# Value stage of a product-key layer: 640 instead of 512 columns gathered, and one subtraction moved from VectorE to GpSimd

## The chip, the cores and the metric

The kernel runs on one core of a Trainium2 chip. The core has TensorE (PE, matrix products), VectorE (DVE), ScalarE (ACT), GpSimd (POOL, which here also issues the indirect DMAs), SyncE (SP, which issues the plain DMAs) and 16 DMA engines. The metric is the device time of one execution in microseconds, lower is better.

## The reference

The whole program is one gMLP block, one stick-breaking attention block, one mixer of convolution and mLSTM, and at the end a layer with product keys ("PEER"), for 256 tokens of width 2048 in float32. The change touches only the last part, the value side of that layer:

```python
def peer_ffn(h, wq, keys, u, v):            # u, v: (N_EXPERTS = 16384, D = 2048)
    ...                                      # 8 heads x 16 experts are chosen for each token
    gate = jax.nn.softmax(top_s, axis=-1)
    ue = jnp.take(u, eid, axis=0)
    act = jax.nn.gelu(jnp.einsum('thkd,td->thk', ue, xt), approximate=False)
    ve = jnp.take(v, eid, axis=0)
    return jnp.einsum('thk,thkd->td', gate * act, ve)
```

Each token thus adds 128 rows of the value table `v`, each with its own weight `gate * act`. Then `h = layernorm(ALPHA * h + ff)` is the output.

## The kernel before

The first 2560 us or so are the earlier blocks, the choice of experts and the gather of rows of `u` (the "ring stage", line 564 for the gathers and line 1853 for the dot products). The weights are then scattered with one-hot matrices (lines 929 and 1840) into a dense table `wT`, 256 tokens by 16384 experts. What follows is called the value stage here.

The value stage splits the 2048 columns of `v` in two. The first 1536 (`V_DENSE`) go through TensorE: the whole table is streamed in 128 chunks of 128 experts, and each chunk is multiplied with the 128 experts' column of `wT`. The last 512 (`V_GATHERED`) are gathered: for each token the 128 chosen rows, one pick at a time for 128 tokens, which VectorE multiplies by the weight and adds.

TensorE has fp32r products (float32 operands rounded to fewer bits), so each operand is used as a rounded part and the rest, and a chunk is three products for each of two token tiles: rounded weights by rounded values, rest of the weights by rounded values, rounded weights by rest of the values. With three banks of 512 columns these are 18 matmuls. Weights and values of even and odd chunks have two buffers (slot `s`).

Each engine's work for chunk c, with the functions' names:

- SP, `load_v`: two transfers of 128 x 768 from the table into `v_raw`, each once the same half of chunk c - 2 was subtracted (`v_lo`).
- ScalarE, `round_w` (waits until TensorE is done with chunk c - 2, then line 1228 writes the rounded weights) and `round_v` (line 1235, two halves).
- VectorE, in `stream_v`: `lo_w` (line 1931, rest of the weights, 128 x 256, two inputs), then twice `lo_v` (line 1938, rest of half a chunk of values) and `weigh` (line 1917, one gathered pick; even picks are added into `h`, odd ones into `v_odd`). Two picks go with one chunk, so that 256 picks (2 tiles of 128) end with the 128 chunks. After every eight picks `stage` (line 1825) copies the next eight row numbers into `idx`.
- GpSimd: the gathers of line 578, each into one of four `v_rows`, once the pick four before it has been weighed (`v_used`). It reads its row numbers from `idx`. After the first tile it also loads two rows of parameters (1 MB each).
- TensorE, `multiply_v` (line 945), waits for `w_hi` and `v_hi`, after six matmuls for `w_lo`, after twelve for `v_lo`.

Each engine executes its own queue in the order in which it is written, so an instruction that waits holds all behind it on that engine. After the last chunk VectorE adds what TensorE has summed (line 1967), and the layer norm ends the kernel.

Of the kernel before, what the change touches and what calls it, by code (L numbers as in the profile page):

```python
# [41 lines left out]
D = 2048  # L42
# [21 lines left out]
GROUP_HEADS = 2  # L64
TILE_GROUPS = PEER_HEADS // GROUP_HEADS
GROUP_PICKS = GROUP_HEADS * TOPK
V_PARTS = 4
V_GATHERED = D // V_PARTS
V_DENSE = D - V_GATHERED
V_BANKS = V_DENSE // BANK  # L70
V_SLOTS = 4
V_HALVES = 2
V_HALF = V_DENSE // V_HALVES
# [70 lines left out]

def build(nc, x, norm_g, a_w_in, a_v_norm_g, a_w_s, a_b_s, a_w_out, b_w_in, b_w_out, final_g, ln_in_g_2, ln_in_b_2,
          w_in_2, b_gate_2, conv_w_2, conv_b_2, mh_norm_g_2, w_out_2, ln1_g_2, ln1_b_2, peer_wq_2, peer_keys_2,
          peer_u_2, peer_v_2, ln2_g_2, ln2_b_2, out):
    NTH, FILL = number_units()
    FIRST, CHUNKS = number_chunks()

# [1 line left out]
    with ctx:  # L152
# [284 lines left out]
        @block.sync  # L437
        def _(sp):
            for b in range(2):
                cut = slice(b * COLS, (b + 1) * COLS)  # L440
                sp.dma_start(h[:, :, cut], x[0].rearrange("(t p) d -> p t d", p=P)[:, :, cut])\
                    .then_inc(loaded[f"x{b}"], 16)

            def load_block(w, c, col, kts=KT):
                for k in range(kts):
                    if not (isinstance(c, int) and c + k < RAW_SLOTS):

                        sp.wait_ge(split_done, c + (k + 1 - RAW_SLOTS))
                    sp.dma_start(w_raw[:, k % RAW_SLOTS, :], w[k * P:(k + 1) * P, bass.ds(col, COLS)])\
                        .then_inc(raw_landed[k % RAW_SLOTS], 16)  # L450

            def load_pairs(w, stage, col, pairs):
                c = FIRST[stage + "0"]
                with sp.Fori(0, pairs) as i:
                    for n in range(2):
                        load_block(w, i * (2 * KT) + (c + n * KT), i * (2 * COLS) + (col + n * COLS))

            for n in range(4):
                load_block(a_w_in[0], FIRST[f"gmlp_v{n}"], GMLP_W + n * COLS)
            load_pairs(a_w_in[0], "gmlp_u", 0, 2)  # L460
            load_pairs(a_w_in[0], "gmlp_z", 2 * GMLP_W, 2)
            for n in range(2):
                load_block(a_w_out[0], FIRST[f"gmlp_out{n}"], n * COLS, 2 * KT)
            load_pairs(b_w_in[0], "att_q", 0, 4)
            load_pairs(b_w_out[0], "att_out", 0, 1)
            for name, (_, b) in MIX_IN.items():
                load_block(w_in_2[0], FIRST[name], b * COLS)
            load_pairs(w_out_2[0], "mix_out", 0, 1)
            load_pairs(peer_wq_2[0], "peer_q", 0, 1)

            def load_v(c, s):

                if s == 1 and isinstance(c, int):

                    sp.wait_ge(scattered, TOKENS // SCATTER + 2)
                for b in range(V_HALVES):
                    cut = slice(b * V_HALF, (b + 1) * V_HALF)
                    if not isinstance(c, int):
                        sp.wait_ge(v_lo, c * V_HALVES + (b + 1 - 2 * V_HALVES))
                    sp.dma_start(v_raw[s][:, cut], peer_v_2[0, bass.ds(c * N_KEYS, N_KEYS), cut])\  # L480
                        .then_inc(v_raw_landed[s][b], 16)

            sp.wait_ge(keys_known, TILES)
            for s in range(2):
                load_v(s, s)
            with sp.Fori(1, N_KEYS // 2) as i:
                for s in range(2):
                    load_v(i * 2 + s, s)
            for n in range(2 * TILES):
                t, b = divmod(n, 2)  # L490
                cols_ = slice(b * COLS, (b + 1) * COLS)
                sp.wait_ge(out_ready, n + 1)
                sp.dma_start(out[0, t * P:(t + 1) * P, cols_], h[:, t, cols_]).then_inc(y_stored, 16)
            sp.wait_ge(y_stored, 2 * 16 * TILES)
# [3 lines left out]
        def _(pool):  # L498
# [54 lines left out]
            with pool.Fori(0, TILES * PICKS // BODY) as i:  # L553
                for n in range(BODY):
# [11 lines left out]
                        in_offset=bass.IndirectOffsetOnAxis(ap=idx[:, b, s:s + 1], axis=0),  # L566
                    ).then_inc(row_landed[s], 16)

            for t in range(TILES):
                with pool.Fori(0, PICKS // BODY) as i:  # L570
                    for n in range(BODY):
                        b, s = divmod(n, GATHER_SLOTS)
                        if s == 0:
                            pool.wait_ge(idx_ready[b], i + ((TILES + t) * PICKS // BODY + 1))

                        pool.wait_ge(v_used, i * BODY + (t * PICKS + n + 1))
                        pool.nop(nofuse=True)
                        nc.gpsimd.indirect_dma_start(  # L578
                            out=v_rows[n % V_SLOTS][:, :], out_offset=None,
                            in_=peer_v_2[0].rearrange("e (s d) -> (e s) d", s=V_PARTS),  # L580
                            in_offset=bass.IndirectOffsetOnAxis(ap=idx[:, b, s:s + 1], axis=0),
                        ).then_inc(v_landed[n % V_SLOTS], 16)
                if t == 0:
                    pool.wait_ge(v_products, D // P)
                    row(row_g2[:, :], ln2_g_2[0], "rows_ln2")
# [4 lines left out]
        def _(pe):  # L590
# [681 lines left out]
        def _(dve):  # L1272
# [620 lines left out]
            for n in range(GROUPS_IN_ALL):  # L1893
# [3 lines left out]
                    keys_of(0)  # L1897
                if n + 2 == GROUPS_IN_ALL:

                    step(v.tensor_scalar(eid[:, ALL:2 * ALL], eid[:, 0:ALL], float(V_PARTS), V_PARTS - 1.0, ALU.mult,  # L1900
                                         ALU.add))
                    step(v.memset(eid[:, 2 * ALL:], 0))
                    keys_of(1)
                finish_gate(n)
# [20 lines left out]
                dve.wait_ge(v_used, (t + 1) * PICKS + V_SLOTS)  # L1925
                step(v.tensor_tensor(h[:, t, V_DENSE:], h[:, t, V_DENSE:], v_odd[:, :], ALU.add))

            def lo_w(c, s):

                dve.wait_ge(w_hi, c + 1)  # L1930
                v.tensor_tensor(w_x[s][:, 1, :, :, :], wT[:, :, bass.ds(c, 1), :], w_x[s][:, 0, :, :, :].bitcast(F32),
                                ALU.subtract).then_inc(w_lo, 1)

            def lo_v(c, s, b):

                cut = slice(b * V_HALF, (b + 1) * V_HALF)
# [8 lines left out]
            def stream_v(t):  # L1945

                with dve.Fori(0, PICKS // BODY) as i:
                    for n in range(BODY // 2):
                        c = i * (BODY // 2) + (t * (N_KEYS // TILES) + n)
                        lo_w(c, n % 2)  # L1950
                        for b in range(V_HALVES):
                            lo_v(c, n % 2, b)
                            weigh(t, i, t * PICKS + 2 * n + b)
# [6 lines left out]


            for t in range(TILES):
                v.bn_stats(bn[:, t, V_BANKS, :], h[:, t, V_DENSE:])
            dve.wait_ge(v_products, N_KEYS)
            for t in range(TILES):
                dst = h[:, t, 0:V_DENSE]
                step(v.scalar_tensor_tensor(out=dst, in0=dst, scalar=ALPHA, in1=flat[t][:, 0:V_DENSE], op0=ALU.mult,
                                            op1=ALU.add))
                for n in range(V_BANKS):
                    ins = v.bn_stats(bn[:, t, n, :], h[:, t, n * BANK:(n + 1) * BANK])  # L1970
                step(ins)
                step(tile_moments(t))
# [12 lines left out]

_INS = ["x", "norm_g", "a_w_in", "a_v_norm_g", "a_w_s", "a_b_s", "a_w_out", "b_w_in", "b_w_out", "final_g", "ln_in_g_2",
        "ln_in_b_2", "w_in_2", "b_gate_2", "conv_w_2", "conv_b_2", "mh_norm_g_2", "w_out_2", "ln1_g_2", "ln1_b_2",
        "peer_wq_2", "peer_keys_2", "peer_u_2", "peer_v_2", "ln2_g_2", "ln2_b_2"]


# [15 lines left out]
```

## Time and profile before

| | |
|---|---|
| median of 3 runs | 3186.89 us (3186.21 to 3187.88) |
| the profiled execution | 3189.3 us, its span 3187.6 us |
| busy over the span | PE 75%, DVE 70%, ACT 35%, POOL 24% |
| value stage | from about 2634 us to 3165 us of the span |
| bytes moved | 766.51 MB, 240 GB/s over the span |

How to read it: PE, DVE, ACT, POOL are the busy times of the engines; a DMA share is the time that packets took on the core's 16 DMA engines as a share of 16 engines' time in that stretch. Queue q1 holds the transfers that SP issues, queue q0 those that GpSimd issues, the gathers among them. The duration of an indirect DMA on POOL is the time that GpSimd spends on issuing it; its time to landing is given apart. Durations of one VectorE operation after another overlap by some 0.1 us, so the cadence is read from their starts. The granted clock of TensorE is 1.00 at its upper level.

### The profile page before, as it was taken

The page shows a single profiled execution, that of the slowest core. Times are in us where ns is not written, and L with a number is a line of the kernel's source. Part 1 is how long each engine was busy: PE and PEld are TensorE (multiplying, and loading weights), DVE is VectorE, ACT ScalarE, POOL GpSimd, SP SyncE. Part 2 cuts the span into 40 slices and gives each one's busy share as a digit, 9 for nine tenths or more (in the row PEclk, how much of TensorE's full clock was granted, in tenths as well). Part 3 has the DMA queues.
Part 4 walks back from the last instruction along what each step waited for, and adds up shares of the span by engine and source line. Part 5 has one row for each costly group of instructions (what it writes and reads, how often), then busy time and mean ns, then how long its engine had stood idle before and what let it go on. Part 6 is the DMA issues. An engine that isn't in the chain of part 4 may idle for free.

```text
span 3187.6 us, 33891 instructions
## 1 busy us (share of the span) xinstructions
PE 2394.3 (75%) x10945; PEld 2000.4 (63%) x10945; DVE 2242.5 (70%) x2950; ACT 1111.3 (35%) x1197; POOL 763.3 (24%) x548
## 2 busy tenths in 40 slices
PE   7999999999999998999998900000111149999997
PEld 5888888888888886888886700000111147887885
DVE  4456455555444556455656699999999998888888
ACT  4444344444444543343443300000000024444443
POOL 1000000000000000000000076665565614455543
PEclk8999999999999998899999955555555589999998
DMA  7655555555656354555564498888897928999996
GB/s 246 195 186 185 178 179 191 185 192 185 185 185 185 124 194 139 164 162 166 187 221 155 172 403 369 362 362 354 316 379 306 391 78 294 320 317 331 322 323 230
DMA packets 183123, 766.51 MB, mean 240 GB/s; under 512 B 22172, under 2 KB 22224, under 8 KB 149104
## 3 DMA queue, kind: packets, MB, share of 16 engines
q1 hardware_dynamic: 123232, 415.29, 40.3%
q0 software_dynamic: 59792, 349.90, 28.0%
q8 instruction: 62, 1.02, 0.1%
q14 instruction: 37, 0.30, 0.0%
HBM read 763.00 MB, written 2.10 MB: 240 GB/s over the span
## 4 chain that ended last, share of the span: by engine, by line
PE 69%; DVE 22%; issue 5%; DMA 2%; ACT 1%; DVEq 1%; POOL 0%; SPq 0%; ACTq 0%; POOLq 0%
PE half L604 50%; PE half L945 15%; DVE ring L1853 14%; DVE onehot_a L1840 2%; PE half L623 1%; DMA w_raw<-in_a_w_in 1%; DMA v_raw<-in_peer_v 1%; DVE onehot_b L1836 1%; PE half L800 1%; DVEq L1840 0%; PE half L672 0%; DMA v_rows<-in_peer_v,idx 0%; DVE left L1751 0%; PE half L903 0%; DVE onehot L1794 0%
## 5 line engine op out<-in xcount | busy, mean ns | idle before, releaser
L604 PE MATMUL half<-w_split,xT 128*128 128x512 f32 x7104 | 1639.0, 392 | 15.2 <-DVE xT L1302 12.6
L604 PEld LDWEIGHTS half<-w_split,xT 128*128 128x128 f32 x7104 | 1337.9, 189 | 294.5 <-issue 8.6
L1283 DVE TENSOR_TENSOR w_split<-w_raw,w_split 128x1024 fp32r<-128x1024 f32 x592 | 722.5, 1225 | 764.1 <-ACT w_split L985 763.3
L985 ACT ACTIVATE w_split<-w_raw 128x1024 fp32r<-128x1024 f32 x592 | 626.6, 1059 | 943.4 <-PE half L604 914.1
L564 POOL DMA_INDIRECT ring<-in_peer_u,idx x256 | 480.9, 1879 | 439.5 <-DVE dots L1853 186.2
L1853 DVE CUSTOM_DVE_ANT_0 ring<-ring,h 128x2048 f32<-128x2048 f32 x256 | 570.0, 2285 | 5.0 <-issue 2.5
L945 PE MATMUL half<-v_split,w_x 128*128 128x512 f32 x2304 | 526.8, 391 | 6.1 <-ACT v_split L1235 4.4
L945 PEld LDWEIGHTS half<-v_split,w_x 128*128 128x128 f32 x2304 | 434.4, 189 | 98.3 <-issue 5.6
L929 PE MATMUL half<-onehot_a,onehot_b 128*128 128x128 f32 x512 | 94.9, 361 | 334.9 <-DVE onehot_a L1840 334.9
L578 POOL DMA_INDIRECT v_rows<-in_peer_v,idx x256 | 266.7, 1042 | 330.2 <-DVE h L1917 208.5
L929 PEld LDWEIGHTS half<-onehot_a,onehot_b 128*128 128x128 f32 x512 | 87.8, 267 | 342.2 <-DVE onehot_a L1840 342.2
L502 POOL DMA_DIRECT2D row_a<-in_final_g x1 | 0.5, 531 | 1130.6 <-DVE ao L1509 1130.6
L1938 DVE TENSOR_TENSOR v_split<-v_raw,v_split 128x768 fp32r<-128x768 f32 x256 | 244.3, 954 | 19.6 <-ACT v_split L1235 19.1
L1235 ACT ACTIVATE v_split<-v_raw 128x768 fp32r<-128x768 f32 x256 | 211.0, 839 | 42.0 <-DMA v_raw<-in_peer_v 39.2
L1219 ACT ACTIVATE wT<-half 128x1024 f32 x32 | 32.8, 1024 | 395.5 <-PE half L929 395.5
L918 PE MATMUL half<-ident,wgt 128*128 128x128 f32 x2 | 0.9, 474 | 186.2 <-DVE wgt L1869 186.2
L918 PE MATMUL half<-ident,pick_keys 128*128 128x128 f32 x4 | 1.0, 354 | 184.1 <-DVE v_odd L1883 184.1
L1228 ACT ACTIVATE w_x<-wT 128x256 fp32r (+1 forms) x128 | 53.4, 418 | 231.4 <-PE half L945 231.4
L918 PEld LDWEIGHTS half<-ident,wgt 128*128 128x128 f32 x2 | 0.4, 182 | 186.8 <-DVE wgt L1869 186.8
L918 PEld LDWEIGHTS half<-ident,pick_keys 128*128 128x128 f32 x4 | 0.6, 175 | 184.3 <-issue 184.3
L1917 DVE SCALAR_TENSOR_TENSOR v_odd<-v_rows,wgt,v_odd 128x512 f32<-128x512 f32 x128 | 95.6, 747 | 16.7 <-DMA v_rows<-in_peer_v,idx 15.8
L1917 DVE SCALAR_TENSOR_TENSOR h<-v_rows,wgt,h 128x512 f32<-128x512 f32 x128 | 95.5, 746 | 7.0 <-DMA v_rows<-in_peer_v,idx 7.0
(287 smaller groups left out, 1152.8 us busy)
## 6 DMA issues: line engine op xcount, KB each, us to landing
w_raw<-in_a_w_in SPq DMA_DIRECT2D x192, 512.0 KB, 3.5
v_raw<-in_peer_v SPq DMA_DIRECT2D x256, 384.0 KB, 5.4
w_raw<-in_b_w_in SPq DMA_DIRECT2D x128, 512.0 KB, 3.5
w_raw<-in_w_in SPq DMA_DIRECT2D x112, 512.0 KB, 3.5
w_raw<-in_a_w_out SPq DMA_DIRECT2D x64, 512.0 KB, 3.5
w_raw<-in_b_w_out SPq DMA_DIRECT2D x32, 512.0 KB, 4.3
w_raw<-in_w_out SPq DMA_DIRECT2D x32, 512.0 KB, 4.6
w_raw<-in_peer_wq SPq DMA_DIRECT2D x32, 512.0 KB, 4.3
```

Source lines behind the costliest of these rows:

```text
L564: nc.gpsimd.indirect_dma_start(out=ring[:, s, :], out_offset=None, in_=peer_u_2[0], in_offset=bass.IndirectOffsetOnAxis(ap=idx[:, b, s:s + ...
L578: nc.gpsimd.indirect_dma_start(out=v_rows[n % V_SLOTS][:, :], out_offset=None, in_=peer_v_2[0].rearrange("e (s d) -> (e s) d", s=V_PARTS), ...
L604: last = mm(ps[half][:, 2 * t + n, :], xt[:, xp, kk, tok], w_split[:, s, wp, n * BANK:(n + 1) * BANK], start=(k == 0 and xp == 0 and wp == ...
L929: last = mm(by_128[s][:, n, :], onehot_b[:, s, n, :], onehot_a[:, s, n, :], start=True, stop=True)
L945: ins = mm(ps[t][:, n, :], w_x[s][:, xp, 1 - t, 0, :], v_split[s][:, vp, n * BANK:(n + 1) * BANK], start=first and xp + vp == 0, stop=last ...
L985: fn(w_split[:, k % SPLIT_SLOTS, 0, :], w_raw[:, k % RAW_SLOTS, :], ACT.Copy).then_inc(hi_done, 1)
L1235: fn(v_split[s][:, 0, cut], v_raw[s][:, cut], ACT.Copy).then_inc(v_hi, 1)
L1283: v.tensor_tensor(w_split[:, s, 1, :], w_raw[:, k % RAW_SLOTS, :], w_split[:, s, 0, :].bitcast(F32), ALU.subtract).then_inc(split_done, 1)
L1840: ins = v.tensor_scalar(onehot_a[:, s, n, :], iota_keys[:, :], picksT[:, 0, bass.ds(token + n, 1)], picksT[:, 2, bass.ds(token + n, 1)], A ...
L1853: v.tensor_tensor_reduce(out=ring[:, s, :], in0=ring[:, s, :], in1=h[:, t, :], scale=1.0, scalar=0.0, op0=ALU.mult, op1=ALU.add, accum_out ...
L1917: v.scalar_tensor_tensor(out=acc, in0=v_rows[m % V_SLOTS][:, :], scalar=wgt[:, bass.ds(i * BODY + m, 1)], in1=acc, op0=ALU.mult, op1=ALU.a ...
L1938: v.tensor_tensor(v_split[s][:, 1, cut], v_raw[s][:, cut], v_split[s][:, 0, cut].bitcast(F32), ALU.subtract).then_inc(v_lo, 1)
```

## The change

640 columns are gathered and 1408 go through TensorE, in banks of 512, 512 and 384 columns. The table is handed to the kernel as two arrays, 1408 and 640 columns wide, where before one array of 2048 columns served both. `lo_w` is taken out of VectorE's loop and written into GpSimd's, behind every second gather.

```diff
-V_PARTS = 4
-V_GATHERED = D // V_PARTS
+V_GATHERED = 640
 V_DENSE = D - V_GATHERED
-V_BANKS = V_DENSE // BANK
+V_BANKS = tuple((lo, min(BANK, V_DENSE - lo)) for lo in range(0, V_DENSE, BANK))
...
-                    sp.dma_start(v_raw[s][:, cut], peer_v_2[0, bass.ds(c * N_KEYS, N_KEYS), cut])\
+                    sp.dma_start(v_raw[s][:, cut], peer_v_dense[0, bass.ds(c * N_KEYS, N_KEYS), cut])\
...
+            def lo_w(c, s):
+
+                pool.wait_ge(w_hi, c + 1)
+                nc.gpsimd.tensor_tensor(w_x[s][:, 1, :, :, :], wT[:, :, bass.ds(c, 1), :],
+                                        w_x[s][:, 0, :, :, :].bitcast(F32), ALU.subtract).then_inc(w_lo, 1)
...
-                            in_=peer_v_2[0].rearrange("e (s d) -> (e s) d", s=V_PARTS),
+                            in_=peer_v_rest[0],
                             in_offset=bass.IndirectOffsetOnAxis(ap=idx[:, b, s:s + 1], axis=0),
                         ).then_inc(v_landed[n % V_SLOTS], 16)
+                        if n % 2:
+                            lo_w(i * (BODY // 2) + (t * (N_KEYS // TILES) + n // 2), n // 2 % 2)
...
-                    for n in range(V_BANKS):
-                        ins = mm(ps[t][:, n, :], w_x[s][:, xp, 1 - t, 0, :], v_split[s][:, vp, n * BANK:(n + 1) * BANK],
+                    for lo, width in V_BANKS:
+                        ins = mm(flat[t][:, lo:lo + width], w_x[s][:, xp, 1 - t, 0, :], v_split[s][:, vp, lo:lo + width],
...
-                    step(v.tensor_scalar(eid[:, ALL:2 * ALL], eid[:, 0:ALL], float(V_PARTS), V_PARTS - 1.0, ALU.mult,
-                                         ALU.add))
+                    step(v.tensor_copy(eid[:, ALL:2 * ALL], eid[:, 0:ALL]))
...
                         c = i * (BODY // 2) + (t * (N_KEYS // TILES) + n)
-                        lo_w(c, n % 2)
                         for b in range(V_HALVES):
                             lo_v(c, n % 2, b)
                             weigh(t, i, t * PICKS + 2 * n + b)
```

GpSimd, the start of the value stage's loop, before (a DMA into `v_rows` is a gather, `v_used` counts weighed picks):

```order
L576 ISA [waits idx_ready0]
L578 DMA v_rows_161<-in_peer_v,idx 128x512 [waits v_used]
L576 REGISTER_ALU
L578 DMA v_rows_162<-in_peer_v,idx 128x512 [waits v_used]
L576 REGISTER_ALU
L578 DMA v_rows_163<-in_peer_v,idx 128x512 [waits v_used]
L576 REGISTER_ALU
L578 DMA v_rows_164<-in_peer_v,idx 128x512 [waits v_used]
```

The same place after the change:

```order
L581 ISA [waits idx_ready0]
L583 DMA v_rows_161<-in_peer_v_rest,idx 128x640 [waits v_used]
L581 REGISTER_ALU
L583 DMA v_rows_162<-in_peer_v_rest,idx 128x640 [waits v_used]
L570 ISA
L571 ISA [waits w_hi]
L571 TENSOR_TENSOR w_x_157<-wT,w_x_157 128x256
L581 REGISTER_ALU
L583 DMA v_rows_163<-in_peer_v_rest,idx 128x640 [waits v_used]
L581 REGISTER_ALU
L583 DMA v_rows_164<-in_peer_v_rest,idx 128x640 [waits v_used]
```

The subtraction for chunk c, with its wait for ScalarE's rounded weights (`w_hi`), now stands between the gathers of picks 2c, 2c + 1 and those of picks 2c + 2, 2c + 3.

VectorE, one chunk in its loop before:

```order
L1931 TENSOR_TENSOR w_x_157<-wT,w_x_157 128x256
L1937 ISA
L1938 TENSOR_TENSOR v_split_159<-v_raw_155,v_split_159 128x768
L1913 REGISTER_ALU
L1915 REGISTER_ALU
L1917 ISA
L1917 SCALAR_TENSOR_TENSOR h<-v_rows_161,wgt,h 128x512
L1937 REGISTER_ALU
L1938 TENSOR_TENSOR v_split_159<-v_raw_155,v_split_159 128x768
L1915 REGISTER_ALU
L1917 ISA
L1917 SCALAR_TENSOR_TENSOR v_odd<-v_rows_162,wgt,v_odd 128x512
```

and after:

```order
L1938 TENSOR_TENSOR v_split_159<-v_raw_155,v_split_159 128x704
L1919 REGISTER_ALU
L1921 REGISTER_ALU
L1923 ISA
L1923 SCALAR_TENSOR_TENSOR h<-v_rows_161,wgt,h 128x640
L1937 REGISTER_ALU
L1938 TENSOR_TENSOR v_split_159<-v_raw_155,v_split_159 128x704
L1921 REGISTER_ALU
L1923 ISA
L1923 SCALAR_TENSOR_TENSOR v_odd<-v_rows_162,wgt,v_odd 128x640
```

Four operations instead of five are left for a chunk, the two of `lo_v` narrower and the two of `weigh` wider.

## Rows read from the trace of the kernel before

**Rows 1.** Chain that ended last: start us, us, what.

```profile
2644.80 210.00 PE half L945 x918
...
2916.27 249.18 PE half L945 x1098
...
3165.48 1.76 DVE h L1967
```

**Rows 2.** Busy time by stretch: columns as its first line names them.

```profile
core 0: us, PE busy (x) PEld busy (x) DVE busy (x) ACT busy (x) POOL busy (x), PEclk, DMA share, GB/s
2440.00:2540.00 100.00, 15.87 (x69) 14.50 (x68) 98.19 (x124) 5.24 (x6) 72.78 (x38) 0.53 0.97 382
2650.00:2850.00 200.00, 200.00 (x884) 165.66 (x883) 176.65 (x256) 96.70 (x147) 94.22 (x97) 1.00 0.95 319
2920.00:3160.00 240.00, 240.00 (x1060) 198.73 (x1059) 211.91 (x309) 117.80 (x178) 120.78 (x117) 1.00 0.93 320
```

**Rows 3.** Groups by line, 2920 to 3160 us: busy, mean ns, idle before.

```profile
L945 PE MATMUL half<-v_split,w_x 128*128 128x512 f32 x1060 | 240.4, 389 | 0.0
L945 PEld LDWEIGHTS half<-v_split,w_x 128*128 128x128 f32 x1059 | 198.8, 188 | 41.3
...
L1938 DVE TENSOR_TENSOR v_split<-v_raw,v_split 128x768 fp32r<-128x768 f32 x118 | 112.6, 955 | 8.6 <-ACT v_split L1235 8.3
...
L1931 DVE TENSOR_TENSOR w_x<-wT,w_x 128x256 fp32r<-128x256 f32 x59 | 24.9, 423 | 8.1 <-ACT w_x L1228 6.9
L1228 ACT ACTIVATE w_x<-wT 128x256 fp32r x59 | 24.7, 419 | 113.2 <-PE half L945 113.2
```

**Rows 4.** DMA queues and issues, 2920 to 3160 us: packets, MB, share; landing us.

```profile
q1 hardware_dynamic: 16806, 45.87, 58.1%
q0 software_dynamic: 9444, 30.94, 34.8%
...
v_raw<-in_peer_v SPq DMA_DIRECT2D x115, 384.0 KB, 5.4
v_rows<-in_peer_v,idx POOLq DMA_INDIRECT x117, 5.8
```

**Rows 5.** DMA queues, 2650 to 2850 us.

```profile
q1 hardware_dynamic: 14042, 38.35, 59.6%
q0 software_dynamic: 7779, 25.50, 35.7%
```

**Rows 6.** Timeline of VectorE from 2638 us: start, length, operation.

```profile
2638.04 0.95 DVE L1938 TENSOR_TENSOR v_split<-v_raw,v_split 128x768 fp32r<-128x768 f32 x1
2638.91 0.74 DVE L1917 SCALAR_TENSOR_TENSOR h<-v_rows,wgt,h 128x512 f32<-128x512 f32 x1
2639.57 0.95 DVE L1938 TENSOR_TENSOR v_split<-v_raw,v_split 128x768 fp32r<-128x768 f32 x1
```

**Rows 7.** Timeline of POOL in the same stretch.

```profile
2638.56 1.25 POOL L578 DMA_INDIRECT v_rows<-in_peer_v,idx  x1 [0.58 <-issue]
2640.42 0.95 POOL L578 DMA_INDIRECT v_rows<-in_peer_v,idx  x1 [0.61 <-issue]
```

**Rows 8.** Timeline of POOL at 2895 us, issues back to back.

```profile
2895.61 0.94 POOL L578 DMA_INDIRECT v_rows<-in_peer_v,idx  x1 [0.30 <-issue]
```

**Rows 9.** Groups by line, 2460 to 2540 us (ring stage).

```profile
L1853 DVE CUSTOM_DVE_ANT_0 ring<-ring,h 128x2048 f32<-128x2048 f32 x31 | 69.2, 2283 | 0.5 <-issue 0.3 <-DVE gate L1821 0.3
L564 POOL DMA_INDIRECT ring<-in_peer_u,idx x31 | 59.4, 1916 | 25.2 <-DVE dots L1853 14.7 <-issue 10.5
```

**Rows 10.** Groups of POOL, 0 to 60 us: its compute instructions.

```profile
L512 POOL MEMSET ones<- 128x256 f32 x1 | 0.3, 312 | 0.1
L509 POOL TENSOR_SCALAR_AFFINE_SELECT upto<-upto 128x128 f32<-128x128 f32 x1 | 0.3, 294 | 0.1
```

**Rows 11.** Timeline around one chunk at 3043 us.

```profile
3043.18 0.42 ACT L1228 ACTIVATE w_x<-wT 128x256 fp32r x1 [1.65 <-PE half L945]
...
3044.36 0.96 DVE L1938 TENSOR_TENSOR v_split<-v_raw,v_split 128x768 fp32r<-128x768 f32 x1 [0.20 <-ACT v_split L1235]
```

More of the change, by code:

```diff
@@ L146, in build @@
           w_in_2, b_gate_2, conv_w_2, conv_b_2, mh_norm_g_2, w_out_2, ln1_g_2, ln1_b_2, peer_wq_2, peer_keys_2,
-          peer_u_2, peer_v_2, ln2_g_2, ln2_b_2, out):
+          peer_u_2, peer_v_dense, peer_v_rest, ln2_g_2, ln2_b_2, out):
     NTH, FILL = number_units()
@@ L1926, in fold @@
                 step(v.tensor_tensor(h[:, t, V_DENSE:], h[:, t, V_DENSE:], v_odd[:, :], ALU.add))
[L1928 to L1932, printed above, removed]
             def lo_v(c, s, b):
@@ L1962, in _ @@
             for t in range(TILES):
-                v.bn_stats(bn[:, t, V_BANKS, :], h[:, t, V_DENSE:])
+                v.bn_stats(bn[:, t, len(V_BANKS), :], h[:, t, len(V_BANKS) * BANK:])
             dve.wait_ge(v_products, N_KEYS)
@@ L1968, in _ @@
                                             op1=ALU.add))
-                for n in range(V_BANKS):
+                for n in range(len(V_BANKS)):
                     ins = v.bn_stats(bn[:, t, n, :], h[:, t, n * BANK:(n + 1) * BANK])
@@ L1987 @@
         "ln_in_b_2", "w_in_2", "b_gate_2", "conv_w_2", "conv_b_2", "mh_norm_g_2", "w_out_2", "ln1_g_2", "ln1_b_2",
-        "peer_wq_2", "peer_keys_2", "peer_u_2", "peer_v_2", "ln2_g_2", "ln2_b_2"]
+        "peer_wq_2", "peer_keys_2", "peer_u_2", "peer_v_dense", "peer_v_rest", "ln2_g_2", "ln2_b_2"]
 def kernel(**inputs):
@@ L1997 @@
     arrays, args = {}, []
+    inputs["peer_v_dense"] = inputs["peer_v_2"][:, :, :V_DENSE]
+    inputs["peer_v_rest"] = inputs["peer_v_2"][:, :, V_DENSE:]
     for name in _INS:
```

## The prediction

> **What bounds the kernel now.** I began with the chain that ended last. In the value stage it is TensorE nearly all the time: 918 matmuls without a break, then after a disturbed stretch of about 60 us another 1098, and then VectorE's closing sums at 3165.48 [rows 1]. So one chunk of 18 matmuls takes 249.18 / 1098 x 18 = 4.085 us, and the 128 chunks 523 us. The second view, busy time by stretch, shows what lies just under that bound: while PE is busy 240.0 of 240 us, VectorE is busy 211.9 and the DMA engines 0.93 of their time (0.95 in the first tile), with POOL at half [rows 2]. ScalarE's rounding of the weights waits 113.2 us for TensorE in those 240 us, which says again that TensorE sets the pace [rows 3]. The granted clock is 1.00, the upper level of 2.4 GHz [rows 2]. The question is therefore not what TensorE saves but which of the three others is met first when its time per chunk falls.
>
> All sums below are for one chunk. They are times 128 for the stage.
>
> **TensorE.** Six of 18 matmuls shrink from 512 to 384 columns. One of 512 takes 4.085 / 18 = 0.227 us. In proportion one of 384 takes 0.170, and the chunk 12 x 0.227 + 6 x 0.170 = 3.74 us. If a matmul can't be shorter than its weight load (188 ns, [rows 3]) it is 12 x 0.227 + 6 x 0.188 = 3.85. I take 3.79, since the fixed part of a matmul doesn't shrink. Alone this would be 128 x 0.295 = 38 us less.
>
> **VectorE.** The two widths of the same subtraction, 955 ns for 768 columns and 423 ns for 256 [rows 3], give 1.04 ns a column. From start to start `lo_v` takes 2638.91 - 2638.04 = 0.87 us and `weigh` 2639.57 - 2638.91 = 0.66 us [rows 6]. After: `lo_v` 0.87 - 64 x 0.00104 = 0.80, `weigh` 0.66 + 128 x 0.00104 = 0.79, the subtraction of the weights gone, so 2 x 0.80 + 2 x 0.79 = 3.2 us, with the copies of row numbers some 3.3. VectorE has room.
>
> **The DMA engines.** Dense bytes fall to 1408 / 1536 = 0.917 of before, gathered bytes rise to 640 / 512 = 1.25: 0.721 + 0.655 = 1.376 MB a chunk in place of 1.311, 5% more. The queues' shares in the quiet part of the second tile are 58.1% and 34.8% [rows 4], in the first 59.6% and 35.7% [rows 5]. Both queues' time goes with bytes at first sight, so after the change the same 4.085 us would hold 58.1 x 0.917 + 34.8 x 1.25 = 96.8%, by the first tile's rows 59.6 x 0.917 + 35.7 x 1.25 = 99.3%. Engines filled to the last would then need 3.95 or 4.06 us. The highest share that a long stretch of this kernel shows is 0.97, in the ring stage, where nothing but gathers ran [rows 2]; at 0.97 it is 4.08 to 4.18 us. There is one unknown. The 117 gathers of 128 rows came in 9444 packets [rows 4], which after the 16 small ones of each gather is half as many as rows, so two rows of 2048 bytes travel in one packet. Whether two of 2560 bytes do, nothing shows. If they travel singly, at the time per byte of the dense queue (58.1 / 45.87 against 34.8 / 30.94 share per MB, 13% more), the share is 53.3 + 43.5 x 1.13 = 102%, so 4.18 us full and 4.3 at 0.97. From below: nothing here shows that time per byte falls for a longer row by more than the ring stage's, 0.97 at 382 GB/s against 0.93 at 320 [rows 2], 13% less per byte; that would make it 53.3 + 43.5 x 0.87 = 91% and 3.72 us full. I take 4.20 us, close to the middle of 4.08 and 4.3, as the row nearest to the case is the present gather. This is the term that decides: what TensorE gives up, the DMA engines don't let it keep.
>
> **GpSimd.** Its new work is one subtraction of 128 x 256 a chunk. No two-input instruction of POOL is in the trace. Below, a write of the same shape takes 0.312 us; above, four of the one-input 128 x 128 passes at 0.294 us would be 1.18 us [rows 10]. I take 0.65: twice 0.294 for one input, a little more for the second. The Trainium skill, GPSIMD Engine Reference, "Engine selection", calls GpSimd about two times slower than VectorE for a two-input elementwise operation; twice VectorE's 423 ns is 0.85 by that page, an estimate, and no run here shows it yet.
>
> A gather's issue takes 0.94 us and 0.30 before it when it follows another [rows 8]. Bare, the chunk is 0.65 + 2 x 1.24 + some 0.15 for the wait = 3.3 us, within the chunk.
>
> The wait that is added: `lo_w` of chunk c waits for the rounded weights, which ScalarE writes when TensorE is done with chunk c - 2 (call that T), ready at T + 0.42 [rows 11]. Queued behind it on POOL are the gathers of picks 2c + 2 and 2c + 3, whose buffers were free long before. They start at about T + 0.42 + 0.1 + 0.65 + 0.30 = T + 1.5, and the second at T + 2.7. Before they started once the pick four earlier was weighed, a chunk sooner. They land 5.8 us after their issue [rows 4]: T + 7.3 and T + 8.5, a little more with a wait for the port below. VectorE comes to `weigh` of them, at its earliest, at T + 4.2 + 2.0 = T + 6.2 (its first `lo_v` starts 3044.36 - 3043.18 = 1.2 us after T, [rows 11]). So VectorE will wait some 1.1 us a chunk for rows, and pushes on until it runs about one more operation behind. TensorE needs the chunk's last `lo_v` two thirds through that chunk, at T + 2 x 4.2 + 2.5 = T + 10.9, and it is done at 7.3 + 0.8 + 0.8 = T + 8.9. The loop from one `lo_w` through landing, `weigh`, `lo_v`, the last third of the matmuls and ScalarE back to `lo_w` three chunks on is 0.65 + 0.3 + 5.8 + 0.8 + 0.8 + 1.3 + 0.4 + 0.5 = 10.5 us, 3.5 a chunk. It costs nothing by itself; it would at a landing above 7.9 us.
>
> **The rest.** At the start gathers 2 and 3 come only after the first `lo_w`, where four used to be issued ahead: 2 us, once. The closing sums (1.76 us twice for 1536 columns, [rows 1]) save 0.3 us together. The multiply-and-add on the row numbers becomes a copy, nothing.
>
> **The sum.** 128 x (4.20 - 4.085) = +15, +2 at the start: 3189.3 + 17 = 3206 us of the profiled execution, which stands 2.4 us above the median of the runs; so 3204. With 4.08 to 4.3 for the chunk it is 3188 to 3217.
>
> **Rival one: TensorE keeps its gain.** If the time of packets per byte falls with longer rows and shorter queues, the chunk comes to between TensorE's 3.79 and 4.0 us. For it: the ring stage moved 382 GB/s [rows 2], and at 3.92 us only 351 are needed. Against it: those rows are 8192 bytes long and there was no second queue. With 3.92: 128 x -0.165 + 2 = -19, 3168 us.
>
> **Rival two: what is saved is what is lost.** The DMA engines hold the chunk at 4.06 to 4.13, by chance the place of the old bound: 3184 to 3193, about 3188. For it stands 4.08, the low end of my own DMA term.
>
> **Rival three: GpSimd and the port that it shares with VectorE.** An issue at 2638.56, begun while `lo_v` ran, took 1.25 us, and one at 2640.42, as the next `lo_v` ended, 0.95 [rows 6, 7]: the first seems to have been held 0.3 us until VectorE changed operations. In the ring stage, with operations of 2.28 us, an issue takes 1.92 us on the mean in place of 0.94 [rows 9]. So GpSimd's reads wait for VectorE's running two-input operation, and the new subtraction reads two operands. Three such waits a chunk, of up to 0.8 us and 0.4 on the mean, make POOL's 3.3 us into 4.5, and the gathers, in order behind each other, can't go faster. The chunk at 4.45 gives 128 x 0.365 + 2 = +49 and 3236 us. It decides from a sum of waits above 0.9 us a chunk. Against it: `lo_w` comes at T + 0.5 to T + 1.2, just where VectorE pauses before its first `lo_v` at T + 1.2 [rows 11], and VectorE has 0.9 us a chunk free. If VectorE is held by the subtraction too it needs 3.3 + 0.65 = 3.95, still below 4.2. The Trainium skill, SBUF — State Buffer, "Who interferes with whom", says that a VectorE instruction with two SBUF inputs contends with a GpSimd instruction that reads SBUF and that the one that comes second blocks fully. The trace agrees for the reading of row numbers, 1.92 against 0.94 us. By that rule all four VectorE operations of a chunk stand in the way, which is what this rival counts.
>
> **How the numbers follow.** The DMA engines pace the stage at more than 4.13: 0.43, with 3204 the likeliest. Rival two 0.20, rival one 0.20, rival three 0.17. A measurement of this kernel can tell about 0.2% (6.4 us) from no change, so slower is 0.43 + 0.17 = 0.60, the same 0.20, faster 0.20. The range leaves out a tenth on each side: below, the stronger half of rival one; above, a chunk beyond 4.5 us. That is 3166 to 3244.
>
> **What would show it.** Right: the chunk near 4.2 us, DMA share 0.95 or more in the value stage, TensorE no longer busy all through but waiting for ScalarE's `v_split`, which waits for `v_raw`, and VectorE waiting for `v_rows`. Rival one: PE busy through the stretches, 360 GB/s. Rival three: DMA share under 0.93, gathers' issues and the subtraction on POOL with means well above 0.94 and 0.65 us, POOL almost without idle time. My working is wrong where matmuls of 384 columns take as long as those of 512, where the subtraction on POOL exceeds 1.2 us, or where gathers land in less time than before although more is moved.

## The result and the profile after

The changed kernel takes 3219.02 us (median of 4 runs, 3217.80 to 3225.34), the kernel before 3187.39 in the same comparison. The ratio is 1.0105, interval 1.009 to 1.012: slower by 31.6 us at the medians, 33 by the ratio. The forecast was 3204, 17 us slower; the sign was right, the loss nearly twice as large.

The loss lies in the value stage alone. Between the last matmul of the first chunk and that of the last, 526.6 us before (2638.4 to 3165.0) became 557.6 (2638.2 to 3195.8). A chunk takes 4.39 us on the mean in place of 4.15, both with the disturbed stretch in the middle; undisturbed it was 4.08 before.

Busy time by stretch, changed kernel (columns as in [rows 2]):

```profile
2650.00:2850.00 200.00, 185.43 (x837) 151.02 (x837) 174.45 (x199) 90.22 (x139) 155.16 (x141) 1.00 0.94 320
2920.00:3160.00 240.00, 224.12 (x1002) 182.49 (x1003) 209.42 (x238) 107.11 (x167) 184.92 (x166) 0.99 0.93 317
```

TensorE is no longer busy all through, at the same granted clock. The DMA engines are no fuller than in [rows 2] and move no more per second; at 0.94 and 0.93 they stay under the 0.97 of the ring stage, so they are not filled all through. VectorE is as busy as before although an operation a chunk went, and POOL went from half to over three quarters.

Groups by line of the changed kernel, 2920 to 3160 us, to be held against [rows 3]:

```profile
L952 PE MATMUL half<-v_split,w_x 128*128 128x512 f32 x668 | 214.4, 402 | 17.6 <-ACT v_split L1242 10.3 <-DVE v_split L1938 6.8
...
L583 POOL DMA_INDIRECT v_rows<-in_peer_v_rest,idx x111 | 133.5, 1203 | 50.1 <-issue 20.0 <-DVE v_odd L1923 16.8 <-DVE h L1923 9.9
L952 PE MATMUL half<-v_split,w_x 128*128 128x384 f32 x334 | 112.9, 338 | 0.0
L1938 DVE TENSOR_TENSOR v_split<-v_raw,v_split 128x704 fp32r<-128x704 f32 x112 | 111.2, 993 | 0.5 <-ACT v_split L1242 0.5
L1242 ACT ACTIVATE v_split<-v_raw 128x704 fp32r<-128x704 f32 x111 | 87.7, 792 | 77.4 <-DMA v_raw<-in_peer_v_dense 76.2
L1923 DVE SCALAR_TENSOR_TENSOR v_odd<-v_rows,wgt,v_odd 128x640 f32<-128x640 f32 x56 | 57.9, 1034 | 11.0 <-DMA v_rows<-in_peer_v_rest,idx 10.5
L571 POOL TENSOR_TENSOR w_x<-wT,w_x 128x256 fp32r<-128x256 f32 x55 | 52.9, 961 | 9.7 <-ACT w_x L1235 9.0
L1923 DVE SCALAR_TENSOR_TENSOR h<-v_rows,wgt,h 128x640 f32<-128x640 f32 x56 | 52.4, 936 | 19.1 <-DMA v_rows<-in_peer_v_rest,idx 18.6
```

The matmul of 384 columns is shorter as hoped (338 ns against 389 in [rows 3]). The subtraction on GpSimd has a mean of 961 ns. ScalarE waits 76.2 us for `v_raw`. Who waited for whom before, in the same stretch:

```profile
DVE v_odd L1917 <- DMA v_rows<-in_peer_v,idx: 11.0, 15, 1.2
...
ACT v_split L1235 <- DMA v_raw<-in_peer_v: 7.8, 23, 0.9
```

So the wait of ScalarE for table data grew tenfold and VectorE's for gathered rows from 11.0 to 29.1 us, while the transfers land as fast as before (issues of the changed kernel, 2920 to 3160 us, against [rows 4]):

```profile
v_raw<-in_peer_v_dense SPq DMA_DIRECT2D x112, 352.0 KB, 5.2
v_rows<-in_peer_v_rest,idx POOLq DMA_INDIRECT x111, 5.9
```

5.2 and 5.9 us, before 5.4 and 5.8. Data that land as fast but are waited for longer were asked for later. For the gathers the timelines show it directly. If each gather is paired with the weighing that frees its buffer (the k-th gather with the weighing four before it), the time from the end of that weighing to the start of the issue has a median of 0.77 us before and 1.14 us after, a mean of 0.85 and 1.27 (2650 to 3140 us). The chain of waits from 2650 to 3140 us, by line, says the same; the changed kernel:

```profile
by line: DMA v_rows<-in_peer_v_rest,idx 28.3%; issue 19.9%; DMA v_raw<-in_peer_v_dense 15.0%; PE half L952 9.8%; DVE v_split L1938 9.4%; POOL v_rows L583 4.6%; DVE h L1923 3.4%; DVE v_odd L1923 2.9%; ACT v_split L1242 2.0%; POOL w_x L571 1.
```

and the kernel before:

```profile
by line: PE half L945 88.7%; DMA v_raw<-in_peer_v 3.0%; DMA v_rows<-in_peer_v,idx 2.6%; issue 2.2%; POOL v_rows L578 1.0%; DVE v_split L1938 0.8%; DVE h L1917 0.5%; ACT v_split L1235 0.3%; DVE w_x L1931 0.2%; DVE v_odd L1917 0.2%; ACT w_x L
```

TensorE's share falls from 88.7% to 9.8%. Most of the chain now runs through round trips: gather, weigh, next gather, and `v_raw` in between.

### The profile page after: what moved, and what is told of

Read it like the earlier page. It is cut to its first block, busy times and chain, and to the rows that moved or that the text cites. A ratio compares the mean times of both kernels' runs of the same rounds, so it can differ in the third digit from the quotient of the medians.

```text
span 3218.5 us, 33891 instructions
## 1 busy us (share of the span) xinstructions
PE 2383.2 (74%) x10945; PEld 1985.8 (62%) x10945; DVE 2262.1 (70%) x2822; ACT 1105.8 (34%) x1197; POOL 924.3 (29%) x676
## 4 chain that ended last, share of the span: by engine, by line
PE 56%; DVE 25%; DMA 8%; issue 8%; ACT 2%; POOL 1%; DVEq 1%; POOLq 0%; SPq 0%; ACTq 0%
PE half L611 50%; DVE ring L1860 14%; DMA v_rows<-in_peer_v_rest,idx 5%; DMA v_raw<-in_peer_v_dense 2%; PE half L952 2%; DVE onehot_a L1847 2%; DVE v_split L1938 2%; PE half L630 1%; POOL v_rows L583 1%; DMA w_raw<-in_a_w_in 1%; DVE onehot_b L1843 1%; DVE h L1923 1%; DVE v_odd L1923 1%; PE half L807 1%; DVEq L1847 0%
## 5 line engine op out<-in xcount | busy, mean ns | idle before, releaser
L952 PE MATMUL half<-v_split,w_x 128*128 128x512 f32 (+1 forms) x2304 | 515.7, 381 | 47.7 <-ACT v_split L1242 26.7
L952 PEld LDWEIGHTS half<-v_split,w_x 128*128 128x128 f32 x2304 | 419.8, 189 | 143.5 <-issue 40.6
L583 POOL DMA_INDIRECT v_rows<-in_peer_v_rest,idx x256 | 304.3, 1189 | 108.4 <-issue 49.8
L1242 ACT ACTIVATE v_split<-v_raw 128x704 fp32r<-128x704 f32 x256 | 202.2, 792 | 175.2 <-DMA v_raw<-in_peer_v_dense 172.2
L1938 DVE TENSOR_TENSOR v_split<-v_raw,v_split 128x704 fp32r<-128x704 f32 x256 | 253.2, 989 | 4.0 <-ACT v_split L1242 3.3
L1923 DVE SCALAR_TENSOR_TENSOR h<-v_rows,wgt,h 128x640 f32<-128x640 f32 x128 | 118.4, 925 | 53.6 <-DMA v_rows<-in_peer_v_rest,idx 52.1
L571 POOL TENSOR_TENSOR w_x<-wT,w_x 128x256 fp32r<-128x256 f32 x128 | 123.5, 965 | 95.0 <-ACT w_x L1235 93.3
L1923 DVE SCALAR_TENSOR_TENSOR v_odd<-v_rows,wgt,v_odd 128x640 f32<-128x640 f32 x128 | 133.3, 1042 | 24.8 <-DMA v_rows<-in_peer_v_rest,idx 23.9
```

What stands on the lines that cost most here:

```text
L571: nc.gpsimd.tensor_tensor(w_x[s][:, 1, :, :, :], wT[:, :, bass.ds(c, 1), :], w_x[s][:, 0, :, :, :].bitcast(F32), ALU.subtract).then_inc(w_ ...
L583: nc.gpsimd.indirect_dma_start(out=v_rows[n % V_SLOTS][:, :], out_offset=None, in_=peer_v_rest[0], in_offset=bass.IndirectOffsetOnAxis(ap= ...
L952: ins = mm(flat[t][:, lo:lo + width], w_x[s][:, xp, 1 - t, 0, :], v_split[s][:, vp, lo:lo + width], start=first and xp + vp == 0, stop=las ...
L1242: fn(v_split[s][:, 0, cut], v_raw[s][:, cut], ACT.Copy).then_inc(v_hi, 1)
L1923: v.scalar_tensor_tensor(out=acc, in0=v_rows[m % V_SLOTS][:, :], scalar=wgt[:, bass.ds(i * BODY + m, 1)], in1=acc, op0=ALU.mult, op1=ALU.a ...
L1938: v.tensor_tensor(v_split[s][:, 1, cut], v_raw[s][:, cut], v_split[s][:, 0, cut].bitcast(F32), ALU.subtract).then_inc(v_lo, 1)
```

## The experiments

All are compared with the kernel before on the same chip, whose medians lay between 3185.3 and 3187.7 us; ratios with their 95% intervals.

**Each part alone: e1, e2, e3.**

e1_pool_only, on the kernel before:

```diff
+                        if n % 2:
+                            lo_w(i * (BODY // 2) + (t * (N_KEYS // TILES) + n // 2), n // 2 % 2)   # on GpSimd
-                        lo_w(c, n % 2)                                                             # on VectorE
```

> The kernel before (512 columns gathered, one array) with the subtraction of the rounded weights on GpSimd. Theory D, that the DMA engines set the pace of the changed kernel: no byte is added here, so the time stays at 3187 us within 6. Theory P, that GpSimd's order and the port it shares with VectorE set it: slower by at least 15 us, 3202 to 3225, with operations of VectorE longer than 0.95 and 0.75 us on the mean.

Measured 3211.69 us, 1.0081 (1.0064 to 1.0099): 24 us lost without a byte more.

e2_cols_only, on the changed kernel, the reverse of that diff.

> The changed kernel (640 columns, two arrays) with the subtraction of the weights back on VectorE. Theory D: the DMA share over the chunk is unchanged, so most of the loss stays, 3204 to 3219 us. Theory P: the loss goes, 3175 to 3192 us.

Measured 3204.77 us, 1.0065 (1.0046 to 1.0084): 17 us lost with VectorE doing the subtraction. This is what my term for the columns had forecast for the whole change. Theory D fails on e1 and theory P on e2: each part costs by itself, and 24 and 17 are more than the 31.6 of both together.

e3_arrays_only, as e2 with `V_GATHERED = 512`.

> The kernel before in every width (512 columns gathered, 1536 through TensorE, subtraction on VectorE), but with the table as two arrays. Both theories: 3187 us within 4. If the layout itself changes how fast packets go, the time per byte of a queue moves by more than 3%.

Measured 3185.85 us, 0.9994 (0.9984 to 1.0004). The two arrays are free. Transfers land 0.6 us sooner than in [rows 4] (4.8 and 5.2), over 2650 to 3140 us only 0.3 and 0.4 sooner (5.0 and 5.3 against 5.3 and 5.7), which the time doesn't show.

**What the subtraction on GpSimd costs by: e4, e12, e6, e7, e13, e14.** Three suspects: the wait for rounded weights in front of the gathers, GpSimd's time, and reads through the port that VectorE needs.

e4_later, on the changed kernel:

```diff
-                        if n % 2:
-                            lo_w(i * (BODY // 2) + (t * (N_KEYS // TILES) + n // 2), n // 2 % 2)
+                        if n % 2 and n > 1:
+                            lo_w(i * (BODY // 2) + (t * (N_KEYS // TILES) + n // 2 - 1), (n // 2 - 1) % 2)
+                        if n == BODY - 1:
+                            lo_w(i * (BODY // 2) + (t * (N_KEYS // TILES) + n // 2), n // 2 % 2)
```

> The changed kernel with GpSimd's subtraction written one pair of gathers later (behind the gathers of picks 2c+2 and 2c+3, except in the last chunk of eight), so that its wait no longer holds them. If the order on GpSimd's queue is what costs (late gathers): 10 to 25 us less than 3219. If the port is, or theory D: 3214 to 3222 us.

Measured 3213.98 us, 1.0085 (1.0068 to 1.0103), 5 below the changed kernel: under what order alone was to bring. The edit has a cost of its own. The subtraction now comes two gathers later, and TensorE waits for it: 11.5 us in 14 waits between 2650 and 3140 us, where the changed kernel has no wait of TensorE for GpSimd. So e4 doesn't price the order alone.

e12_pool_later, the same edit on e1_pool_only.

> e1_pool_only (512 columns, subtraction on GpSimd) with the subtraction written one pair of gathers later, so its wait for the rounded weights doesn't hold them. If e1's 24 us come from the gathers held behind that wait: 3187 to 3197 us. If they come from GpSimd and VectorE holding each other up at the shared port: 3206 us or more.

Measured 3211.14 us, 1.0077 (1.006 to 1.0093), as e1. With the wait moved behind the gathers (in all but the last chunk of eight) nothing is won, so that wait is not the only cause. TensorE's wait for the later subtraction is small here (2.5 us in 2 waits). What the trace shows besides: POOL has hardly a pause (busy 184.1 of 240 us, another 34.4 idle as "issue" before gathers), and its operations and VectorE's hold each other. Groups by line, 2920 to 3160 us:

```profile
L1942 DVE TENSOR_TENSOR v_split<-v_raw,v_split 128x768 fp32r<-128x768 f32 x113 | 136.3, 1206 | 2.7 <-ACT v_split L1245 1.6
L584 POOL DMA_INDIRECT v_rows<-in_peer_v,idx x114 | 133.8, 1174 | 52.3 <-issue 34.4 <-DVE h L1927 9.1 <-DVE v_odd L1927 8.3
...
L572 POOL TENSOR_TENSOR w_x<-wT,w_x 128x256 fp32r<-128x256 f32 x57 | 51.1, 896 | 4.2 <-ACT w_x L1238 3.1
```

`lo_v` takes 1206 ns, in [rows 3] 955: VectorE stands still 0.5 us a chunk.

e6_write_only, on the kernel before, whose VectorE keeps its subtraction:

```diff
+            def extra(c, s):
+
+                pool.wait_ge(w_hi, c + 1)
+                pool.nop(nofuse=True)
+                nc.gpsimd.memset(scratch[:, s, :], 0.0).then_inc(w_extra, 1)      # 128 x 576
...
+                        if n % 2:
+                            extra(i * (BODY // 2) + (t * (N_KEYS // TILES) + n // 2), n // 2 % 2)
...
+                pe.wait_ge(w_extra, c + 1)
```

> The kernel before, the subtraction still on VectorE; GpSimd at the place where the change puts it waits for the same rounded weights and then writes zeros over 128 x 576 of scratch (no operand read, about 0.6 us), and TensorE waits for that too. Theory P-port (what costs is that GpSimd reads through the port VectorE needs): no loss, 3184 to 3194 us. Theory P-order (what costs is the wait and the time on GpSimd's queue): like e1, 3205 to 3215 us.

Measured 3208.74 us, 1.0062 (1.004 to 1.0085). Reads are not needed for a loss of this size: the wait and the time on GpSimd's queue give it without them.

e7_read_twice, with a subtraction in place of the zeros:

```diff
-                nc.gpsimd.memset(scratch[:, s, :], 0.0).then_inc(w_extra, 1)
+                nc.gpsimd.tensor_tensor(scratch[:, s, 0:2 * P], wT[:, :, bass.ds(c, 1), :].rearrange("p t o k -> p (t o) k"),
+                                        w_x[s][:, 0, :, 0, :].bitcast(F32), ALU.subtract).then_inc(w_extra, 1)
```

> As e6_write_only, but GpSimd does a real two-input subtraction of 128 x 256 into scratch, so it reads as in the changed kernel, and VectorE does its own too. P-port: at least e1's loss, 3208 to 3235 us, VectorE's operations lengthened by 0.6 to 0.8 us once a chunk. P-order: the same as e6 within 4 us.

Measured 3199.92 us, 1.0038 (1.0026 to 1.0051), below both expectations. VectorE's operations are lengthened (odd `weigh` 981 ns against 747), yet the time is not above e6's. I have no explanation for its being the lowest of the family; its interval overlaps those of e6 and e13.

e13_wait_only, on e6: `memset(scratch[:, s, 0:8], 0.0)`.

> e6_write_only with its 128 x 576 of zeros cut to 128 x 8, some 0.1 us, so GpSimd keeps the wait for the rounded weights in front of the gathers and loses almost no time otherwise. Theory O (the wait in order in front of the gathers is what costs): 3200 us or more. Theory G (GpSimd's own time a chunk is what costs: two issues of 0.3 + 1.2 us and the added operation fill the chunk): 3187 to 3195 us.

Measured 3201.36 us, 1.0048 (1.0031 to 1.0065). The wait in front of the gathers, with 0.1 us of work, costs 16 us. TensorE waits for the zeros nowhere in the trace, so the cost comes through the gathers behind the wait. From the end of a weighing to the issue into its buffer it is now 1.13 us at the median and 1.41 on the mean (0.77 and 0.85 before). Who waited for whom, 2920 to 3160 us:

```profile
ACT v_split L1246 <- DMA v_raw<-in_peer_v: 43.2, 51, 2.3
...
DVE h L1928 <- DMA v_rows<-in_peer_v,idx: 21.0, 20, 1.8
...
DVE v_odd L1928 <- DMA v_rows<-in_peer_v,idx: 16.7, 23, 3.7
```

Both waits that grew in the changed kernel grow here too: for rows 37.7 us in place of 11.0, for the table 43.2 in place of 7.8. Nothing was changed about the table's transfers, so their part follows from the late rows.

e14_write_later, e6 with the placement of e4.

> e6_write_only with the same 0.6 us of zeros written one pair of gathers later, so no gather stands behind the wait. Theory O: 3185 to 3193 us. Theory G: like e6, 3200 to 3210 us. Beside e12 (3211 us, the same place with a subtraction that reads) it also gives the price of the reads.

Measured 3205.00 us, 1.0068 (1.0051 to 1.0084). Time on GpSimd, with that wait gone from all but the last chunk of eight and without a read, goes with a loss of 20 us. Part of it is the experiment's own, since TensorE now waits for the later zeros (2650 to 3140 us):

```profile
PE half L957 <- POOL scratch L575: 6.5, 15, 0.9
```

The rest fits late gathers: 1.37 us on the mean from weighing to issue. So the wait by itself gives most of the loss (e13), GpSimd's time some 13 us (an estimate: e14's 20 less the 6.5), and both together (e6) 22: they don't add up. Between e14 and e12, which reads, lie 6 us at the medians, with overlapping intervals. That is not a clean price of the reads, because e12's gathers are less late (1.12 us on the mean) and its VectorE is held instead.

**What 640 columns cost by: e5, e8, e15, e16, e17, e18.** VectorE subtracts in all of these.

e5_short_rows, on e2:

```diff
-                            out=v_rows[n % V_SLOTS][:, :], out_offset=None,
-                            in_=peer_v_rest[0],
+                            out=v_rows[n % V_SLOTS][:, 0:BANK], out_offset=None,
+                            in_=peer_v_short[0],
```

> e2_cols_only with all widths of the engines kept (640 columns weighed, 1408 multiplied, subtraction on VectorE), but each gather carries only 512 of the 640 columns of its rows; the last 128 gathered columns are zeros, so that part of the sum is left out. Bytes of a chunk: 1.245 MB in place of 1.376. Theory D (the bytes hold e2 above TensorE's own time): the chunk falls to about TensorE's 3.84 us and the time to 3155 to 3170 us. If e2's loss is rather in order, buffers' turn or VectorE's wider operations: within 8 us of e2's 3205.

Measured 3186.56 us, 0.9998 (0.9985 to 1.0011), single runs 3172.7 to 3191.8. 18 us come back with the bytes; the 30 us to TensorE's own time don't. Neither expectation holds; the bytes are a part of it. The edit also makes the gathered table narrower, so layout may have a share in the 18. Its most frequent chunk is 3.84 us with all widths of the engines as in e2, so VectorE's wider operations don't by themselves keep e2 above that.

e8_w576, e15_w608, e16_w544, e17_w624: e2 with another `V_GATHERED`.

> 640 replaced by 576 gathered columns (1472 through TensorE in 512, 512, 448), two arrays, subtraction on VectorE. Theory D with a usable share of 0.95: TensorE 3.96 us a chunk, DMA 0.948 x 4.08 / 0.95 = 4.07, so 3183 to 3190 us, no gain from TensorE's shorter work. If instead bytes do not bind, TensorE's time shows: 3168 to 3176 us.

> e8_w576 with 608 columns gathered (1440 = 512, 512, 416 through TensorE), subtraction on VectorE. TensorE's own chunk is 3.90 us; bytes are 1.3% above e8's. If bytes and landings take over between 576 and 640 as e8 and e2 say: 3180 to 3195 us.

> The same with 544 columns (1504 = 512, 512, 480). TensorE's own chunk is 4.02 us and should be filled: 3178 to 3182 us.

> As e15_w608 with 624 columns gathered (1424 = 512, 512, 400 through TensorE), 1.368 MB a chunk. If the loss sets in step by step with bytes and with TensorE's shorter chunk: between the two, 3182 to 3196 us. If it is a step that belongs to 640: within 5 us of e15's 3174.

| gathered columns | kernel | time, us | ratio to before | bytes a chunk, MB |
|---|---|---|---|---|
| 512 | e3 | 3185.85 | 0.9994 (0.9984 to 1.0004) | 1.311 |
| 544 | e16 | 3184.42 | 0.9997 (0.9988 to 1.0007) | 1.327 |
| 576 | e8 | 3176.06 | 0.9964 (0.9950 to 0.9978) | 1.343 |
| 608 | e15 | 3173.73 | 0.9959 (0.9949 to 0.9970) | 1.360 |
| 624 | e17 | 3185.41 | 1.0000 (0.9986 to 1.0014) | 1.368 |
| 640 | e2 | 3204.77 | 1.0065 (1.0046 to 1.0084) | 1.376 |

Theory D failed on 576 columns, which were to bring nothing and bring 10 us; 608 were to lose some of that and don't; 544 were to come to 3178 to 3182 us and stay at 3184. Only 624 came out in its range. 608 and 576 are faster than both kernels of this study. From 608 to 640 the time rises by 31 us at the medians, 34 by the ratios, for 1.2% more bytes, 12 us to 624 and 19 more to 640, so it is a limit that is crossed and not a cost by the byte. Near it the runs scatter: e17's lie between 3174.9 and 3197.0. e15's busy time by stretch refutes the ceiling of 0.95 that e8's expectation used, and the time per byte of my prediction:

```profile
2650.00:2850.00 200.00, 199.56 (x911) 169.55 (x910) 180.07 (x263) 100.51 (x152) 114.62 (x101) 1.00 0.97 342
2920.00:3120.00 200.00, 198.76 (x913) 170.39 (x912) 181.99 (x265) 100.43 (x153) 113.03 (x101) 1.00 0.97 344
```

343 GB/s: at that rate the 1.376 MB of 640 columns would be 4.01 us, and e2 has 4.26 on the mean. TensorE's side of the table is not what was expected either. At 544 columns it is busy all through, yet the chunk is 4.07 or 4.11 us and not 4.02: the matmuls of 480 columns start 218 ns after each other, but those of 512 now take 231 ns where the kernel before has 227. Why isn't known.

e18_pitch, on e2: `inputs["peer_v_2"][:, :, :V_DENSE + 32]` as the dense table.

> e2_cols_only (640 columns, subtraction on VectorE) with the dense table 1440 columns wide, of which 1408 are read, so its rows lie 5760 bytes apart, as in e15, in place of 5632. If the distance between rows makes e2 slow: towards e15's 3174, 3190 us or less. If not: within 5 us of e2's 3205.

Measured 3195.66 us, 1.0028 (1.0018 to 1.0038). Rows 5760 bytes apart in place of 5632 give 9 us back at the medians, neither expectation; nearly a third of the step from 608 to 640 thus goes with the table's layout.

**The two round trips: e9, e10, e11.**

```diff
                         for b in range(V_HALVES):
                             lo_v(c, n % 2, b)
+                        for b in range(V_HALVES):
                             weigh(t, i, t * PICKS + 2 * n + b)
```

> The changed kernel with VectorE's order in a chunk changed from lo_v, weigh, lo_v, weigh to lo_v, lo_v, weigh, weigh. Theory L (late rows hold VectorE, so both halves of v_raw come free late, its next transfer starts late, and ScalarE and TensorE wait for it): v_raw no longer waits behind a late gather of its own chunk, so 10 to 25 us less than 3219. Theory D (bytes alone): within 4 us of 3219.

> e2_cols_only (640 columns, subtraction on VectorE) with the same order lo_v, lo_v, weigh, weigh. Theory L: 8 to 25 us less than e2's 3205, towards TensorE's 3.84 us a chunk. Theory D, bytes alone: within 4 us of 3205.

> e8_w576 with the order lo_v, lo_v, weigh, weigh. Its chunk is already 3.96 to 4.03 us where TensorE alone needs 3.96, so both theories: 0 to 6 us less than 3176.

Measured: e9 3220.31 us (1.0109, 1.0093 to 1.0126), e10 3228.00 (1.0141, 1.0120 to 1.0161), e11 3223.45 (1.0112, 1.0092 to 1.0133). Theory L as I had put it fell: freeing the second half of `v_raw` earlier wins nothing, and e11 is 47 us above e8. What the edit also does is weigh the first of a chunk's two picks one operation, 0.9 us, later, and so issue its successor's gather 0.9 us later. In e11 that is the round trip with the least room (below). The chain of waits of e11, 2650 to 3140 us, by line:

```profile
by line: DMA v_rows<-in_peer_v_rest,idx 46.6%; issue 21.8%; DVE v_split L1936 10.2%; DVE h L1915 5.2%; POOL v_rows L577 4.4%; DVE v_odd L1915 4.0%; DVE w_x L1929 2.1%; DMA v_raw<-in_peer_v_dense 2.1%; DVEq L1915 0.9%; DVEq L1935 0.5%; DVEq 
```

## Why the prediction had the sign right and the mechanism wrong

**TensorE** (3.79 us a chunk): an undisturbed chunk of the changed kernel has 3.84 us, the most frequent value. Right within 0.05. The difference is not in the narrow matmuls, 175 ns from start to start, but in those of 512 columns, 233 ns in place of 227.

**VectorE**: `lo_v` and `weigh` of e2 take 886 and 880 to 886 ns, as worked out. In the changed kernel 993 and 936 to 1034: held up by GpSimd, 86 operations in 112 chunks by more than 0.15 us, for 0.54 us at the median; that is 0.41 us a chunk on the mean. I had priced this (3.95) and found it harmless.

**GpSimd**: 0.65 us a subtraction; the trace has a median of 0.76 and a mean of 0.96. The mean is what its queue pays.

**The step that failed** is the one on the wait that is added: "It costs nothing by itself; it would at a landing above 7.9 us." So in the sum the move of the subtraction stood with the 2 us of the start. e1, that move alone, costs 24 us with gathers that land in 5.7. e13 puts the wait, and nothing else of weight, into the kernel before: 16 us. I had found that rows come some 1.1 us after VectorE wants them and followed only whether TensorE gets its values in time in that chunk. I did not ask what else starts from VectorE. Two transfers do, each with two chunks to come round. Their room can be read from the trace of before, VectorE and POOL at 3045 us:

```profile
3045.24 0.75 DVE L1917 SCALAR_TENSOR_TENSOR h<-v_rows,wgt,h 128x512 f32<-128x512 f32 x1
3045.90 0.95 DVE L1938 TENSOR_TENSOR v_split<-v_raw,v_split 128x768 fp32r<-128x768 f32 x1
...
3046.76 0.94 POOL L578 DMA_INDIRECT v_rows<-in_peer_v,idx  x1 [1.62 <-DVE h L1917]
```

A weighing begins at 3045.24, the gather into its buffer at 3046.76, and lands 5.8 us later [rows 4]: 7.3 us of the 8.16 that two chunks last, 0.8 of room. The table's way round is `lo_v` 0.95, landing 5.4, ScalarE's 0.84, some 0.1 at each handover: 7.4 us, and as much room. A VectorE that runs 1.1 us late, as I had worked out, has used both up. Then ScalarE waits for `v_raw` (7.8 us before, 76.2 after), TensorE for ScalarE, and the late products make the next wait on GpSimd end late too. That the wait makes the gathers late, and that late rows lengthen the waits for the table too, e13 shows. That it is this lack of room through which the delay reaches TensorE is read from the waits and fits e9 to e11, where 0.9 us of delay in the first round trip costs at least what 0.8 freed in the second wins; no run gave a round trip more room by itself, for instance by more row buffers, so this part is argued.

**The DMA term** (4.20 us, "the term that decides") gave the right size for its part, e2's 17 us, but by luck. Its working took each queue's time per byte as fixed and 0.97 as the share that would be reached. The changed kernel reaches 0.94 and 0.93, and the time per byte isn't fixed: at 0.97 the changed kernel's own rows (0.94 at 320 GB/s) would give 4.17 us a chunk, e2's (0.95 at 331) 4.07 and e15's 4.01, a gain. None of these is what the kernels show (4.36 and 4.26 on the mean, 2650 to 3140 us). What e2 seems to meet is again the round trip: at TensorE's 3.84 us two chunks last 7.7 us, a weighing of 0.80 by its start-to-start time, the 0.77 from its end to the issue and landings of 6.0 (median of e2) are 7.6, and landings vary from 4.3 to 7.4. At 608 and 576 the room is 0.4. This is worked out from medians and not tested by a run; e5 (shorter rows, landings of 5.6) fits it as well as it fits a cost of bytes. My upper end, packets that carry one row, didn't come: 115 gathers of e2 are 9215 packets, again two rows each.

**The rivals.** Rival one had the gain for narrower changes: e15 is it at 608 columns. Rival three named the right engine, GpSimd's gathers in order behind each other, and put the price at 49 us with the waits for the port as cause; the waits are there (issues of 1203 ns in place of 1043, the subtraction at 961), but order and time on the queue cost without any read (e13, e14), and what the reads add isn't separated. Rival two's 3184 to 3193 left out the 2 us of the start, which changes nothing here.

**The signs** were a poor guide. TensorE waiting for `v_split`, ScalarE for `v_raw` and VectorE for `v_rows` came as written for a right prediction, since late issues give the same waits as full engines. Of the three signs that were to show a wrong working none came. Only the DMA share under 0.95 and POOL's long operations pointed away from the bytes.

## What to carry to other kernels

When an instruction is moved into the queue of an engine that issues transfers, price the transfers that stand behind it: from the release of a buffer to its next use, against the time until that use, before asking whether the engine has idle time. Here buffers came round with about one operation of room, and the loss set in within 32 columns, so a size is to be swept in small steps (here 544, 576, 608, 624, 640) and one part changed at a time. An experiment that moves an instruction should be checked for a new wait that the move makes, as TensorE's in e4 and e14. Without the move of the subtraction, and with 576 or 608 columns, the same idea gains 10 to 12 us at the medians.

## What the hardware showed that was not expected

- A GpSimd subtraction of 128 x 256 with two inputs takes 0.75 us when nothing holds it (VectorE: 0.42), and up to 1.49 beside VectorE. A VectorE operation that overlaps it can be held for about as long: a `lo_v` of 1.69 us in place of 0.88, begun 0.19 us before a subtraction of 0.74 (changed kernel, at 2817.70 us). Which of the two begins first in the profile doesn't settle which is held: at 2821.93 us a subtraction begun 0.19 us after a `lo_v` took 1.29 us and the `lo_v` its 0.88, while the next weighing, 0.88 by itself, took 1.26.
- A write of 128 x 576 on GpSimd takes 0.59 us and leaves VectorE's durations as they were (951 and 749 ns in e6): here the subtraction, which reads, held VectorE up, and the write didn't.
- With two arrays in place of one landings were 0.3 to 0.6 us shorter at the same bytes (one profile of each), and a dense row pitch of 5760 in place of 5632 bytes made e18 9 us faster than e2.
- A matmul of 512 columns starts 227 ns after the one before where all have 512, and 231 to 233 ns after it where every third has 480 or 384 (e16, the changed kernel), at the same granted clock of 1.00.
- A stretch with gathers and plain transfers mixed can fill 0.97 of the DMA engines at 344 GB/s (e15), 24 GB/s more than the kernel before shows.
